# A gated linear-attention recurrence in a two-block kernel: decay exponents from running sums on VectorE instead of level sums by matrix products

## The reference, cut to what matters

```python
def step(s, inp):                       # one chunk of one direction
    qc, kc, vc, ac = inp
    bcum = jnp.cumsum(ac, axis=2)       # running sums of the log decays
    o_inter = jnp.einsum('bhtd,bhde->bhte', qc * jnp.exp(bcum), s)
    diff = bcum[:, :, :, None, :] - bcum[:, :, None, :, :]
    decay = jnp.exp(jnp.where(mask[:, :, None], diff, -jnp.inf))
    att = jnp.einsum('bhtd,bhsd,bhtsd->bhts', qc, kc, decay)
    o_intra = jnp.einsum('bhts,bhse->bhte', att, vc)
    b_last = bcum[:, :, -1:, :]
    s_new = exp(b_last)[..., None] * s + einsum('bhsd,bhse->bhde', kc * exp(b_last - bcum), vc)
```

## Time and profile before

| what | value |
| --- | --- |
| median of 3 runs | 2241.2 us (2239.53 to 2242.85) |
| the profiled execution | 2238.03 us, its span 2236.2 us |
| TensorE granted clock, mean over the span | 0.994 of full |
| PE busy | 2187.7 us (98%), 13238 products |
| DVE busy | 1484.3 us (66%), 2797 instructions |
| ACT busy | 968.0 us (43%), 1606 instructions |
| POOL busy | 34.2 us (2%), 37 instructions |
| HBM | 287.77 MB read, 129 GB/s over the span |

### The profile page before, as it was taken

How to read it: one execution, slowest core, us unless ns; L and a number is a source line. 1 busy time by engine, 2 the same in 40 slices (tenths; PEclk the granted TensorE clock), 3 DMA queues, 4 the chain that set the end, 5 groups by cost and what they waited for, 6 DMA issues and landing times.

```text
span 2236.2 us, 33908 instructions
## 1 busy us (share of the span) xinstructions
PE 2187.7 (98%) x13238; PEld 1934.3 (86%) x13238; DVE 1484.3 (66%) x2797; ACT 968.0 (43%) x1606; POOL 34.2 (2%) x37
## 2 busy tenths in 40 slices
PE   8899999999999999999999999999999999999998
PEld 6789987788997999988888888888889999979997
DVE  6779888779888567655446543643565766666666
ACT  5664445565445544432225422213245444354343
POOL 0000000000000010000000000000000100000000
PEclk9899999999999999999999999999999999999999
DMA  6457775647775311212331233333313125425653
GB/s 194 125 172 242 239 229 163 197 153 238 239 253 182 114 38 39 57 57 85 95 85 33 72 113 96 94 87 107 118 56 107 49 76 161 122 67 164 185 178 125
DMA packets 195415, 291.03 MB, mean 130 GB/s; under 512 B 9940, under 2 KB 88052, under 8 KB 195000
## 3 DMA queue, kind: packets, MB, share of 16 engines
q1 hardware_dynamic: 193424, 283.89, 41.5%
q10 hardware_dynamic: 1832, 4.98, 0.7%
HBM read 287.77 MB, written 1.06 MB: 129 GB/s over the span
## 4 chain that ended last, share of the span: by engine, by line
PE 84%; DVE 8%; ACT 3%; DVEq 2%; issue 2%; DMA 0%; ACTq 0%
PE bank L2116 23%; PE bank L2118 23%; PE bank L2117 23%; DVE WLO L1033 2%; PE bank L2596 2%; PE bank L2814 1%; PE bank L2838 1%; PE bank L2535 1%; PE bank L2536 1%; PE bank L2618 1%; ACT WHI L526 1%; PE bank L2541 1%; PE bank L2631 1%; PE bank L2337 1%; DVE ATL L1061 1%
## 5 line engine op out<-in xcount | busy, mean ns | idle before, releaser
L526 ACT ACTIVATE WHI<-RAW 128x1024 fp32r<-128x1024 f32 (+2 forms) x500 | 506.1, 1017 | 831.2 <-PE bank L2118 798.8
L1033 DVE TENSOR_TENSOR WLO<-RAW,WHI 128x1024 fp32r<-128x1024 f32 (+2 forms) x500 | 581.0, 1170 | 422.3 <-ACT WHI L526 412.8
L2116 PE MATMUL bank<-ATH,WHI 128*128 128x256 f32 (+1 forms) x2032 | 665.1, 327 | 9.6 <-DVE ATL L1470 2.6
L2118 PE MATMUL bank<-ATH,WLO 128*128 128x256 f32 (+1 forms) x2032 | 652.5, 321 | 0.0
L2117 PE MATMUL bank<-ATL,WHI 128*128 128x256 f32 (+1 forms) x2032 | 652.5, 321 | 0.0
L2116 PEld LDWEIGHTS bank<-ATH,WHI 128*128 128x128 f32 x2032 | 387.3, 191 | 44.1 <-issue 4.1
L2117 PEld LDWEIGHTS bank<-ATL,WHI 128*128 128x128 f32 x2032 | 387.6, 191 | 28.6 <-issue 0.7
L2118 PEld LDWEIGHTS bank<-ATH,WLO 128*128 128x128 f32 x2032 | 387.5, 191 | 28.3
L2116 PE MATMUL bank<-WHI,ATH 128*128 128x512 f32 (+2 forms) x996 | 358.2, 360 | 10.0 <-DVE ARENA L1078 4.7
L2117 PE MATMUL bank<-WLO,ATH 128*128 128x512 f32 (+2 forms) x996 | 352.7, 354 | 0.0
L2118 PE MATMUL bank<-WHI,ATL 128*128 128x512 f32 (+2 forms) x996 | 352.6, 354 | 0.0
(11 more groups left out here) (302 smaller groups left out, 2341.8 us busy)
## 6 DMA issues: line engine op xcount, KB each, us to landing
RAW<-in_w_in SPq DMA_DIRECT2D x192, 512.0 KB, 3.8
RAW<-in_w_ff SPq DMA_DIRECT2D x128, 512.0 KB, 4.6
ARENA<-in_w_ada SPq DMA_DIRECT2D x64, 384.0 KB, 4.8
RAW<-in_o_w_in SPq DMA_DIRECT2D x24, 512.0 KB, 4.2
RAW<-in_e_w_in SPq DMA_DIRECT2D x16, 512.0 KB, 4.8
RAW<-in_w_ple_gate SPq DMA_DIRECT2D x16, 512.0 KB, 3.8
RAW<-in_w_br_gla SPq DMA_DIRECT2D x16, 512.0 KB, 3.5
RAW<-in_w_br_attn SPq DMA_DIRECT2D x16, 512.0 KB, 3.6
```

The costliest lines, as they stand in the source:

```text
L526: nc.scalar.activation(WHI[:, slot, 0:n], RAW[:, slot, 0:n], ACT.Copy).then_inc(hi_split, 1)
L1033: V.tensor_tensor(WLO[:, slot, 0:n], RAW[:, slot, 0:n], WHI[:, slot, 0:n], ALU.subtract).then_inc(lo_split, 1)
L2116: mm(o, ah, bh, start=start, stop=False, skip_group_check=free)
L2118: return mm(o, al, bh, start=False, stop=stop, skip_group_check=free)
```

## The change

`gla_pair`, `gla_last` and their columns of TRI are gone (TRI has 512 columns instead of 2176). ScalarE now also copies the running sums of each tile into SUMS (2 x 512 columns), and VectorE makes the exponents of a level as differences of SUMS at two places, into APART (2 x 512 columns; `gla_apart`, one instruction a level). SUMS and APART lie in the room of CTX, so the context rows are loaded a second time after the recurrence of layer 0, from ScalarE's queue. ScalarE makes the exps of a level in three instructions (one in the last level). The squares and the gains move from VectorE to ScalarE. Some steps change their place in the queues: `gla_pre(i + 1)` before `gla_scores(0, i)`, `gla_min` before `gla_place(0)`, `gla_level(6, i)` before `gla_place(6)`.

```diff
-TRI_TILE, TRI_LEVEL, TRI_LAST = 0, 4 * P, 4 * P + 2 * P * (len(LEVELS) - 1)
-NTRI = TRI_LAST + P
+NTRI = 4 * P
...
+        SUMS = at(8192, 2 * TOK, "p (d n) -> p d n", d=2)
+        APART = at(8192 + 2 * TOK, 2 * TOK, "p (d n) -> p d n", d=2)
...
                 def gla_tiles(*which):
                     for b in which:
-                        exps(P1[:, :, b // 2, b % 2 * S:(b % 2 + 1) * S], two(b % 2))
+                        act.wait_ge(g_diff, T.next(g_diff))
+                        nc.scalar.activation(SUMS[:, 1 - b // 2, b % 2 * S:(b % 2 + 1) * S], bank[b % 2][:, S:2 * S], ACT.Copy)
+                        nc.scalar.activation(P1[:, :, b // 2, b % 2 * S:(b % 2 + 1) * S], two(b % 2), ACT.Exp).then_inc(g_exp, 1)
...
+                def gla_level(i, n):
+                    half, m, room = LEVELS[n], tq // (2 * LEVELS[n]), APART
+                    act.wait_ge(g_apart, T.next(g_apart))
+                    if n >= 2:
+                        act.wait_ge(g_level, (layer * GH + i) * (1 + len(LEVELS)) + n)
+                    if n == len(LEVELS) - 1:
+                        nc.scalar.activation(LASTE[:, :, 0:tq // 2], room[:, :, 0:tq // 2], ACT.Exp).then_inc(g_decay, 1)
+                        return
+                    q, key = (P2[:, n % 2, k, 0:tq].rearrange("p (m e x) -> p e m x", e=2, x=half) for k in range(2))
+                    nc.scalar.activation(q, apart(room, 0, (TOK + half, 2), (2 * half, m), (1, half)), ACT.Exp)
+                    nc.scalar.activation(key[:, 0, :, :], apart(room, TOK, (2 * half, m), (1, half)), ACT.Exp, scale=-1.0)
+                    nc.scalar.activation(key[:, 1, :, :], apart(room, half, (2 * half, m), (1, half)), ACT.Exp, scale=-1.0).then_inc(g_decay, 1)
+
+                def gla_squares(i):
+                    act.wait_ge(g_out, layer * GH + i + 1)
+                    for t in range(nq):
+                        last = nc.scalar.activation(ON[:, t, :], bank[6 + t // 2][:, t % 2 * GDV:(t % 2 + 1) * GDV], ACT.Square, scale=GDV ** -0.5,
+                                                    accum_out=GS[:, t:t + 1])
+                    last.then_inc(g_squared, 1)
...
                 gla_tiles(0, 1, 2, 3)
-                gla_pair(0, 0, 0, 1)
                 gla_turned()
+                gla_level(0, 0)
+                gla_level(0, 1)
                 taken(0, 2)
                 next_hi(0, 1, 2)
-                gla_pair(0, 0, 2, 3)
                 for i in range(GH - 1):
+                    if i:
+                        gla_gains(i - 1)
                     taken(i, 3)
...
                 for u in (2, 3):
                     taken(GH, u)
                     next_hi(GH, u)
                 T.next(gemm_step, (GH + 1) * SLOTS)
-                act.wait_ge(g_turned, (layer + 1) * GH * 2)
+                if layer == 0:
+                    act.wait_ge(g_decay, GH * len(LEVELS))
+                    act.dma_start(CTX, io["ctx_2"][0].rearrange("(t p) n -> p t n", p=P)).then_inc(ctx_in, 16)
+                gla_squares(GH - 1)
+                gla_gains(GH - 1)
...
+                def gla_apart(n):
...
+                    whole, middle = ((TOK, 2), (2 * half, m), (1, 2 * half)), ((TOK - 1, 2), (2 * half, m), (0, 2 * half))
+                    V.tensor_tensor(apart(room, 0, *whole), apart(SUMS, 0, *whole), apart(SUMS, half, *middle), ALU.subtract).then_inc(g_apart, 1)
...
-                    if n % 2 == 0:
-                        dve.wait_ge(g_exp, T.next(g_exp, nq))
+                    dve.wait_ge(g_decay, T.next(g_decay))
+                    gla_apart(n + 1)
...
                     gla_keys(i + 1)
-                    gla_squares()
+                    gla_apart(0)
                     gla_roots()
                     gla_rows()
                     gla_level(0, i + 1)
                     gla_level(1, i + 1)
-                    gla_gains(i)
                     lo(2)
...
                     gla_inter(i)
-                    gla_scores(0, i)
-                    if layer == 0:
-                        gla_pair(i, 1, 0, 1)
                     pe.wait_ge(*outside(i, 3))
                     gla_pre(i + 1)
+                    gla_scores(0, i)
                     gla_scores(1, i)
                     gla_scores(2, i)
...
                     columns(i + 1, 0, 0)
-                    gla_pair(i, 1, 2, 3)
                     columns(i + 1, 0, 1)
                     gla_scores(3, i)
-                    gla_pair(i, 2, 0, 1)
                     gla_scores(4, i)
                     value_tile(i + 1, 0)
-                    gla_pair(i, 2, 2, 3)
                     value_tile(i + 1, 1)
                     gla_scores(5, i)
-                    gla_last(i)
                     gla_scores(6, i)
```

More of the change, by code:

```diff
@@ L326, in mixer_kernel, with apart @@
         rows = [h, CTX]
+        SUMS = at(8192, 2 * TOK, "p (d n) -> p d n", d=2)
+        APART = at(8192 + 2 * TOK, 2 * TOK, "p (d n) -> p d n", d=2)
+        def apart(a, first, *dims):
+            return bass.AP(a.tensor, a.offset + first, [list(a.ap[0])] + [list(d) for d in dims])
         JUNK = at(4096, NT * D, "p (t n) -> p t n", t=NT)
@@ L506, in gla @@
                     nc.gpsimd.tensor_tensor(P1[:, 1, :, 0:tq], P1[:, 1, :, 0:tq], q, ALU.mult).then_inc(g_qb, 1)
-                    T.next(g_exp, steps - 4)
             for layer in range(2):
@@ L789, in gla_logs @@
                     nc.scalar.activation(LOGS, LOGS, ACT.Ln, bias=one).then_inc(g_logs, 1)
-                def exps(dst, src):
-                    act.wait_ge(g_diff, T.next(g_diff))
-                    nc.scalar.activation(dst, src, ACT.Exp).then_inc(g_exp, 1)
                 def two(b):
@@ new lines, in gla_squares, with gla_gains @@
+                def gla_squares(i):
[4 more added lines that the diff above has]
+                    last.then_inc(g_squared, 1)
+                def gla_gains(i):
+                    for c in range(2):
+                        act.wait_ge(g_turned, (layer * GH + i) * 2 + c + 1)
+                        last = nc.scalar.activation(VG[:, 0:nq, bass.ds(i * GDV + c * P, P)], bank[6 + c][:, 0:tq].rearrange("p (t n) -> p t n", t=nq),
+                                                    ACT.Copy, scale=col("gla_norm_g_2", layer * 2 + c))
+                    last.then_inc(g_normed, 1)
@@ L1753, in gla_rows @@
                     last.then_inc(g_rows, 1)
-                def gla_gains(i):
-                    for c in range(2):
-                        dve.wait_ge(g_turned, T.next(g_turned))
-                        last = V.tensor_scalar(VG[:, 0:nq, bass.ds(i * GDV + c * P, P)], bank[6 + c][:, 0:tq].rearrange("p (t n) -> p t n", t=nq),
-                                               col("gla_norm_g_2", layer * 2 + c), None, ALU.mult)
-                    last.then_inc(g_normed, 1)
-                    drain()
                 gla_min(6)
@@ L1836, in gate_z @@
                     drain()
+                    if i == 0:
+                        dve.wait_ge(g_normed, (layer + 1) * GH)
                     gla_times(i, w)
```

134 lines of the change are left out of this document (40 added, 94 removed).

## The result

| | kernel before | changed kernel |
| --- | --- | --- |
| median (5 runs each, same chip, alternating) | 2239.77 us (2237.92 to 2242.85) | 2251.96 us (2249.41 to 2252.11) |
| profiled execution, its span | 2238.03, 2236.2 us | 2251.27, 2249.5 us |
| layer 0's recurrence | 229.21 us | 229.08 us |
| layer 1's recurrence | 162.01 us | 175.73 us |
| TensorE granted clock, mean over the span | 0.994 | 0.989 |

The ratio is 1.005, interval 1.0035 to 1.0064: slower by 0.5%, 12 us. The forecast was 2244.7 with a range of 2229 to 2256; the time lies in the range, 7 us above the forecast. A recurrence is taken from its first product for the logits (`gla_pre`) to the start of its last transposition of rows. Of the 13.3 us between the two spans, 13.6 lie in the recurrences, -1.7 in front of layer 0's, -0.1 between the two and +1.4 behind layer 1's.

The account below looks back on a forecast made before the run. TensorE, busy 98% of the span, was taken as bound only by its own queue. Layer 0's +3.9 and layer 1's -7.4 make the kernel 3.5 us longer: 2241.5 profiled, 2244.7 on the median, range 2229 to 2256.

Parts of the forecast that it names:

- What goes, what comes: Level-sum products leave TensorE, 46 us in all; VectorE's subtractions come, making a level 2.4 us in layer 0, 1.3 in layer 1.
- The sum: All heads and edges added: layer 0 gains 3.9 us, layer 1 loses 7.4, the kernel gets 3.5 longer.
- rival (b): ScalarE's exps become the slower part of levels 1, 3 and 5: +8 us, 2252.5; chance 0.25.
- I to V: Second half of a head, states' products to value products: 30.69 to 28.3 us in layer 0, 20.03 to 21.1 in layer 1.
- V to I: First half of a head, value products to states' products: 20.32 to 21.7 us in layer 0, 16.68 to 17.0 in layer 1.
- The collision with GpSimd: In V to I, VectorE's SBUF work taken as serial with GpSimd's doubling and multiplication; TensorE waits 2.4 us for layer 0's rows.
- Edges: Gains at first head, last head and tail: -2.4, +5.4, -2.2 us in layer 0; -0.7, +0.3, -2.8 in layer 1.
- (a): GpSimd costs nothing, as the small root operations slip into its gaps: -11.4 us, 2233; chance 0.30.
- (c): VectorE's chain stays hidden, TensorE is dense and all 46 us are won: 2195; chance 0.05.
- (d): The second context load or the narrow edits bite: at most 4 us, inside the ranges; no chance of its own.

Follow-up runs that it names:

- e12: Changed kernel with ScalarE making the exponentials of a level's key decays in one instruction, not two: 2250.21 us, ratio 1.0053 to the kernel before.
- e3: Changed kernel plus column sums that nobody reads where TensorE waits in front of scores 5 and 6: 2246.65 us, 1.0040 of the kernel before.
- e4: Changed kernel with GpSimd multiplying only 16 columns of the queries, most of that product left out: 2245.46 us, 1.0035 of the kernel before.
- e7: Changed kernel with GpSimd's multiplication of the queries waiting for VectorE's root operations from the second head on: 2245.77 us, 1.0047 of the kernel before.
- e6: Changed kernel without the second load of the context rows at the end of layer 0's recurrence: 2253.16 us, 1.0072 of the kernel before.
- e11: Changed kernel with the squares back on VectorE, the gains staying on ScalarE: 2258.95 us, 1.0091 of the kernel before.
- e8: Changed kernel plus early table exp, earlier value tile 2 read, unread filling products, squares before last column read, GpSimd's multiplication behind roots: 2225.83 us, 0.9948 of kernel before.
- e10: The kernel of e8 without the products that nobody reads, so four edits on the changed kernel: 2233.11 us, 0.9974 of the kernel before.

## Why the prediction was right, and where it was not

**What goes, what comes.** Right. The products went and VectorE's chain took their place: the subtraction takes 1.21, the pair of multiplications 1.28, a level 2.52 from start to start (909.04 to 911.56), where 2.4 was assumed. The sum has 46.1 us of products go and the kernel get 3.5 longer, so it holds 49.6 us of new waits; TensorE's idle time grew by 40.1. On the other side the lower clock took up to some 14 us more than before (length times one minus clock of the whole recurrences), which the sum does not have, and about 6 us more of the measured 13.6 are in neither. So 9.5 us of waits too many stood against some 20 us not counted, and the miss of 10 is half of what it might have been: that part is luck. So is the place in the range: 2252.0 lies above the forecast's own 2238 to 2251 and inside 2229 to 2256 by the room left for rival (b), whose mechanism e12 rules out.

**I to V.** The waits came where they were put: 0.4 in front of scores 2 (forecast 0.8), 1.97 in front of scores 5 (2.0), 0.91 in front of scores 6 (0.95) in layer 0; 1.0, 1.5 and 0.6 in layer 1, where 1.2, then 0.6, and 0.5 for tile copies had been put. The half took 29.6 (28.3) and 21.9 (21.1). In layer 0 the 1.3 us too many are the clock's (they went when e3 filled the waits: 1.2 and 1.5), in layer 1 they are the wait for scores 5, 0.9 longer than forecast.

**V to I.** The collision with GpSimd is as described, on the subtraction and on one root operation, and e4 and e7 show that it holds the rows up. The half took 20.8 (21.7) and 16.6 (17.0): the wait for rows was 1.5 and not 2.4, and that of the products with the last state in layer 1 0.2 and not 1.0. The doubling had been counted behind the keys with all of its 2.08 us. It starts 0.04 behind the keys (881.47), so those 2.08 most likely hold its own wait for VectorE's 1.22; what is left, 0.86, is also what the subtraction lasted too long (2.06 against 1.22). By the Trainium skill, "SBUF — State Buffer", section "SBUF: two separate sides", whichever of the two engines starts first has the shared ports for its whole instruction and the other is blocked; these rows fit that in both directions, though no run takes the doubling away.

**Edges.** This step failed. The last heads (-4.5 and -0.5, forecast -4.0 and 0) and the tails (+1.2 and +2.2, forecast +2.2 and +2.8) are near, but the first heads cost +4.2 in layer 0 and +8.6 in layer 1 where 0 and +1.8 had been put down. That is 11.0 us, all of the 10.1 by which the recurrences missed (forecast +3.5, measured +13.6), with small errors of both signs in the rest. Most of it lies where the step put 2.4 and 0.7 us, up to the first product with the states: there the first heads lost 5.9 and 6.3. Two waits had been overlooked or mis-sized: the table load behind the copy (1.9), and 2.7 at the outer products, which in layer 1 stands against the 0.7 of the step. The larger part is the clock, 0.91 and 0.85 in this part (before 1.00 and 0.94), up to 3.3 and 3.5 us, which the forecast did not price at all: it counted an idle microsecond of TensorE as one.

**Rivals.** (a), GpSimd costs nothing: wrong, by e4 and e7. (b), ScalarE's exps: its number, 2252.5, is nearly what was measured, but by another mechanism; e12 rules its own out. A level's exps took 1.24 to 1.32 us in layer 0 and 0.80 to 0.85 in layer 1, against the 1.25 and 0.7 of its point and the 1.5 and 1.1 that it assumed, and VectorE's wait for them was 0.17 and 0.2. (c), all hidden: wrong. (d): wrong, by e6 (the DMA share that it rests on is 14 to 23% in the earlier trace rows, not 24). The layer that was to gain did not and the one that was to lose lost more; that the whole gets slower had been given a third of the chances.

## What to carry to other kernels

Work taken from an engine that sets the time buys nothing if the engine then waits for the one that took it over; here 46 us of products went and 12 us were lost. Price a new wait of TensorE twice, as the wait and as the slower products behind it, look at the granted clock in short stretches right behind it, and, where the wait cannot be avoided, try products that nobody reads. In these runs GpSimd's instruction on SBUF cost least beside VectorE instructions that read PSUM. And before a stretch of one run is called a gain, look at how much it differs between runs that leave it alone.

## What the runs showed of the hardware that was not expected

- TensorE's granted clock fell to 0.50 behind waits as short as 1.97 and 0.91 us with eight products between, in a stretch of otherwise dense work, and with 0.8 us more of wait (e11) the middle heads were 1.9 and 3.7 us longer.
- 20 useless products in each of three heads of layer 0 and 14 in layer 1 made the kernel 6 us faster (0.9948 against 0.9974 of the kernel before, e8 against e10).
- One kernel's time went with the mean granted clock of the execution: e10 from 2223.3 us at 0.996 to 2239.5 at 0.988.
- A VectorE operation on 128x4 elements in SBUF took 2.34 us beside a GpSimd multiplication and 0.19 without it (e4); rows with an operand in PSUM took their 1.66 beside the same multiplication (e7).
